# Delta-rule recurrence: the tokens' partition half set by the feature chunk, and state products over four quarters of the array and two PSUM banks

## The reference, cut to what matters

```
sa  = S @ a_t
S   = S * w_t + sa (x) b_t + v_t (x) k_t      # S is 64x64 per head
y_t = S @ r_t
```

## Time and profile before

| what | value |
|---|---|
| median of 3 runs | 1300.0 us (1299.5 to 1301.41) |
| span of the profiled execution | 1299.6 us |
| TensorE busy | 1269.2 us, 98% |
| VectorE busy | 894.2 us, 69% |
| ScalarE busy | 679.4 us, 52% |
| mean granted TensorE clock | 0.995 |
| the stretch of the loop over four chunks | 752.2 to 782.0 us |

### The profile page before, as it was taken

The page is one execution under the profiler, slowest core; times in us unless marked ns, Lnnn a source line. Parts: engine busy times, 40 slices in busy tenths (PEclk is TensorE's granted clock), DMA queues, the critical chain, the costliest instruction groups (busy, mean ns, idle before and its releaser), DMA issues.

```text
span 1299.6 us, 23670 instructions
## 1 busy us (share of the span) xinstructions
PE 1269.2 (98%) x10054; PEld 1098.1 (84%) x10059; DVE 894.2 (69%) x1467; ACT 679.4 (52%) x1228; POOL 83.8 (6%) x103
## 2 busy tenths in 40 slices
PE   9999999999999999999999999999999999999997
PEld 6978888889967888888898997888897987788886
DVE  6886666674685666656898848666668366766666
ACT  6874444463584454544663434444455477445452
POOL 3000500000060000000001600000000000000000
PEclk9999999999999999999999999999999999999999
DMA  9445454544412555553443003654555441455550
GB/s 351 159 184 200 184 190 184 188 188 166 165 62 81 200 195 194 194 195 130 164 161 131 5 36 114 219 193 188 195 194 194 176 161 61 187 194 194 195 194 33
DMA packets 17496, 214.45 MB, mean 165 GB/s; under 512 B 1960, under 2 KB 2128, under 8 KB 4720
## 3 DMA queue, kind: packets, MB, share of 16 engines
q1 hardware_dynamic: 15888, 205.43, 41.9%
q0 software_dynamic: 1504, 7.52, 1.6%
HBM read 211.87 MB, written 1.06 MB: 164 GB/s over the span
## 4 chain that ended last, share of the span: by engine, by line
PE 83%; DVE 9%; ACT 6%; issue 1%; DMA 1%; SPq 0%; DVEq 0%; ACTq 0%
PE psum L696 25%; PE psum L670 14%; PE psum L676 7%; PE psum L486 4%; PE psum L487 4%; PE psum L488 4%; DVE w_low L1996 3%; ACT w_high L1443 2%; PE psum L1054 2%; PE psum L1198 1%; PE psum L585 1%; PE psum L1245 1%; PE psum L1373 1%; PE psum L581 1%; PE psum L577 1%; PE psum L1069 1%
## 5 line engine op out<-in xcount | busy, mean ns | idle before, releaser
L1996 DVE TENSOR_TENSOR w_low<-ring,w_high 128x1024 fp32r<-128x1024 f32 x372 | 443.4, 1227 | 188.5 <-ACT w_high L1443 188.5
L1443 ACT ACTIVATE w_high<-ring 128x1024 fp32r<-128x1024 f32 x372 | 372.7, 1048 | 139.7 <-PE psum L696 105.4
L696 PE MATMUL psum<-w_high,up_split 128*128 128x512 f32 x1024 | 287.6, 391 | 0.8 <-DVE up_split L2151 0.8
L696 PEld LDWEIGHTS psum<-w_high,up_split 128*128 128x128 f32 x1024 | 190.3, 188 | 40.5 <-issue 2.7
L670 PE MATMUL psum<-act_split,w_high 128*128 128x512 f32 x768 | 191.6, 391 | 0.0
L696 PE MATMUL psum<-w_low,up_split 128*128 128x512 f32 x512 | 163.2, 390 | 0.0
L670 PEld LDWEIGHTS psum<-act_split,w_high 128*128 128x128 f32 x768 | 139.6, 189 | 26.0
L1544 ACT ACTIVATE up_split<-work 128x256 fp32r<-128x256 f32 x112 | 46.8, 418 | 159.4 <-DVE work L2144 148.8
L486 PE MATMUL psum<-act_split,w_high 128*128 128x256 f32 x448 | 129.1, 288 | 0.3 <-DVE act_split L2162 0.3
L487 PE MATMUL psum<-act_split,w_high 128*128 128x256 f32 x448 | 126.7, 283 | 0.0
L488 PE MATMUL psum<-act_split,w_low 128*128 128x256 f32 x448 | 126.7, 283 | 0.0
(11 more groups left out here) (360 smaller groups left out, 1873.7 us busy)
## 6 DMA issues: line engine op xcount, KB each, us to landing
ring<-weights SPq DMA_DIRECT2D x95, 2048.0 KB, 7.5
work<-rows POOLq DMA_DIRECT2D x4, 1024.0 KB, 5.1
ring<-weights SPq DMA_DIRECT2D x4, 512.0 KB, 8.4
work<-rows POOLq DMA_DIRECT2D x4, 512.0 KB, 5.4
x<-x_in SPq DMA_DIRECT2D x2, 512.0 KB, 4.7
work<-t_bias POOLq DMA_DIRECT2D x1, 1024.0 KB, 8.4
out<-x SPq DMA_DIRECT2D x4, 256.0 KB, 2.1
con<-consts SPq DMA_DIRECT2D x1, 576.0 KB, 22.0
```

The source lines that it names most:

```text
L696: last = mm(bank(acc[(th, n)]), up_split[:, m, a, P * th:P * th + P], w[:, f], start=start and i == 0, stop=stop and i == len(pairs) - 1, ...
L1443: A(high[:, HIGH_SLOT[name], f], ring[:, n % RING, f], ACT.Copy).then_inc(weights_high, 1)
L1996: V.tensor_tensor(low[:, n % RING, f], ring[:, n % RING, f], high[:, HIGH_SLOT[name], f].bitcast(f32), ALU.subtract).then_inc(weights_spli ...
```

## The change

The partition half of a unit's tokens is now chosen by the feature chunk: `at_half(hf, c)`. In a call that joins features and tokens (g-state, KT, BT, the turn) even chunks use the diagonal quarters and odd chunks the other two, so that one call goes round all four; even chunks write one bank, odd chunks the next (`pair(q)`). Calls whose operands are both on the tokens' side (g-open, u) keep the two diagonal quarters and now alternate over two banks. y keeps one bank: its y-state is split into even chunks, a wait for their completion (`y_even`), and odd chunks, with a further wait (`y_odd`) before y-end. y-open moves behind g-state, y-state moves behind u, and a wait on g-open's own completion (`g_opened`) stands before g-state in chunks 1 to 3 instead of in the odd ones.

`bt` and `kt` are turned by plain 64x64 products, as `vt` was, because pieces beside each other no longer are a pair of neighbouring columns: 64 products a name instead of 31 transposes of 128 columns and two of 64. The Gram matrices are written chunk by chunk; their number, width and alternation of quarters are the same. Readers of a pair of banks use an access pattern of two banks by four pieces of 64.

```diff
-                            if t >= 0:
-                                last = nc.tensor.transpose(got, flat[:, t:t + 2 * CH], cst("diag")[half(hf), :])
...
+                                c, tc = 2 * ((4 * i + j) // NT) + (upper ^ hf), (4 * i + j) % NT
+                                t = (c * NT + tc) * CH
                                 last = mm(psum[half(upper), BANK[q + hf], j * CH:j * CH + CH],
-                                          work[half(hf), src, t:t + CH], cst("center")[half(hf), :], start=True, stop=True)
+                                          work[half(hf), src, t:t + CH], cst(through)[half(hf), :], start=True, stop=True)
...
+                def heads(q, term, first=True, final=True, by_head=False, col=0):
+
                     for c in range(NC):
...
+                        for hf in range(2):
+                            lhsT, rhs = term(half(hf), at_half(hf, c), c)
+                            out, at = at_half(hf, c) if by_head else half(hf), col + c // 2 * CH
+                            last = mm(psum[out, BANK[q] + c % 2, at:at + CH], lhsT, rhs, start=(first and c < 2),
+                                      stop=final, skip_group_check=True)
...
+                def outputs(term, cs=range(NC), first=False, final=False):
+
+                    for c in cs:
+                        for hf in range(2):
+                            lhsT, rhs = term(half(hf), at_half(hf, c), c)
+                            last = mm(psum[half(hf), BANK[y], c * CH:c * CH + CH], lhsT, rhs, start=(first and c == 0),
+                                      stop=final, skip_group_check=True)
...
-                opened = heads(y, [lambda at, hd, c: (rw_gk[at, c, tc, CH:2 * CH], beside(RW_VT, at, hd, c))], True, False)
...
                     pe.wait_ge(sig("state_next"), tc)
...
+                    pe.wait_ge(sig("g_opened"), tc)
+                    heads(q, lambda at, hd, c: (rw_ar[hd, c, tc, 0, :], rw_s[hd, c, :]), False, True)
+                open_bank(y)
+                outputs(lambda at, hd, c: (rw_gk[at, c, tc, CH:2 * CH], beside(RW_VT, at, hd, c)), first=True)
                 read_out(pe, q)
...
+                heads(u, lambda at, hd, c: (rw_y[at, c, tc, :], rw_g[at, c, :]), col=256)
+                if tc:
+                    def from_state(at, hd, c):
+                        return rw_ar[hd, c, tc, 1, :], rw_s[hd, c, :]
+
+                    outputs(from_state, range(0, NC, 2)).then_inc(sig("y_even"), 1)
+                    pe.wait_ge(sig("y_even"), tc)
+                    outputs(from_state, range(1, NC, 2)).then_inc(sig("y_odd"), 1)
...
-                q = TURN[("wkv_g", tc)]
...
-                taken(A(rw_g.rearrange("p c i -> p (c i)"), bank(q), ACT.Copy), q)
+                taken(A(odd_even(rw_g), pair(q), ACT.Copy), q)
```

More of the change, by code:

```diff
@@ L367, in half, with pair, odd_even @@
             return slice(64 * i, 64 * i + 64)
+        def pair(q, at=0):
+            return view(psum[:, BANK[q], at:at + 1], [[512, 2], [CH, NC // 2], [1, CH]])
+        def odd_even(src):
+            return src.rearrange("p (c a) i -> p a c i", a=2)
         def xt(th, n):
@@ L1117, in across, with turned @@
             def across(q, c0, fn, width):
-                n = 1024 // (NT * width)
                 for odd in range(2):
                     open_bank(q + odd)
-                for c in range(n):
-                    for tc in range(NT):
-                        at = (c * 2 + tc // 2) * width
+                for tc in range(NT):
+                    for odd in range(2):
                         for hf in range(2):
-                            lhsT, rhs = fn(half(hf), c0 + c, tc)
-                            last = mm(psum[at_half(hf, tc), BANK[q + tc % 2], at:at + width], lhsT, rhs,
+                            lhsT, rhs = fn(half(hf), c0 + odd, tc)
+                            last = mm(psum[at_half(hf, odd), BANK[q + odd], tc * width:tc * width + width], lhsT, rhs,
                                       start=True, stop=True)
-                        if c == n - 1 and tc >= NT - 2:
+                        if tc == NT - 1:
                             last.then_inc(bank_filled, 1)
[L1132 to L1141, removed]
-                            if t >= 0:
-                                last = nc.tensor.transpose(got, flat[:, t:t + 2 * CH], cst("diag")[half(hf), :])
[L1144 to L1150, removed]
+            def turned(name, src, through="diag"):
                 for i in (0, 2):
@@ L1223, in turn_heads @@
                     for hf in range(2):
-                        last = mm(psum[at_half(hf, tc), BANK[q], c * CH:c * CH + CH], y_norm[half(hf), c, :],
+                        at = c // 2 * CH
+                        last = mm(psum[at_half(hf, c), BANK[q] + c % 2, at:at + CH], y_norm[half(hf), c, :],
                                   cst("diag")[half(hf), :], start=True, stop=True)
@@ L1232, in beside @@
                     hf = hd.start // CH
-                    slot = (c * NT + tc + hf) // 2 % (NC * NT // 2)
+                    slot = c // 2 * NT + tc
                     return work[at, src, (2 * slot + hf) * CH:(2 * slot + hf) * CH + CH]
-                def heads(q, terms, first=True, final=True, by_head=False):
-                    if first:
-                        open_bank(q)
+                def heads(q, term, first=True, final=True, by_head=False, col=0):
                     for c in range(NC):
[L1241 to L1247, removed]
+                        for hf in range(2):
[3 more added lines that the diff above has]
+                                      stop=final, skip_group_check=True)
+                    if final:
+                        last.then_inc(bank_filled, 1)
+                    return last
+                def outputs(term, cs=range(NC), first=False, final=False):
[4 more added lines that the diff above has]
+                                      stop=final, skip_group_check=True)
                     if final:
@@ L1279, in _ @@
                 if tc < NT - 1:
-                    heads(state, [lambda at, hd, c: (beside(RW_BT, at, hd, c), rw_u[at, c, :])], False, True, True)
-                heads(y, [lambda at, hd, c: (rw_gb[at, c, tc, CH:2 * CH], rw_u[at, c, :])], False, True)
+                    heads(state, lambda at, hd, c: (beside(RW_BT, at, hd, c), rw_u[at, c, :]), False, True, True)
+                if tc:
+                    pe.wait_ge(sig("y_odd"), tc)
+                outputs(lambda at, hd, c: (rw_gb[at, c, tc, CH:2 * CH], rw_u[at, c, :]), final=True)
             for n in range(2):
@@ L1846, in _ @@
                 filled(q)
-                taken(A(rw_g.rearrange("p c i -> p (c i)"), bank(q), ACT.Copy), q)
+                taken(A(odd_even(rw_g), pair(q), ACT.Copy), q)
                 q = TURN[("wkv_u", tc)]
                 filled(q)
-                taken(A(rw_u.rearrange("p c i -> p (c i)"), bank(q), ACT.Copy), q)
+                taken(A(odd_even(rw_u), pair(q, 256), ACT.Copy), q)
                 q = TURN[("wkv_y", tc)]
@@ L2594, in heads_out @@
                     filled(q)
-                ins = V.tensor_tensor(raw, bank2(q, NC)[:, c, :], chunks(RW_G)[:, c, t], ALU.mult)
+                ins = V.tensor_tensor(odd_even(raw), pair(q)[:, :, 2 * i:2 * i + 2, :],
+                                      odd_even(chunks(RW_G)[:, c, t]), ALU.mult)
                 if i:
@@ L2613, in _ @@
                     filled(q)
-                    s = rw_s.rearrange("p c i -> p (c i)")
+                    s = odd_even(rw_s)
                     if tc:
-                        taken(V.tensor_tensor(s, s, bank(q), ALU.add), q)
+                        taken(V.tensor_tensor(s, s, pair(q), ALU.add), q)
                     else:
-                        taken(V.tensor_copy(s, bank(q)), q)
+                        taken(V.tensor_copy(s, pair(q)), q)
                     settle()
```

43 lines of the change are left out of this document (18 added, 25 removed).

## The result

The changed kernel takes 1304.98 us (median of 5 runs, 1304.34 to 1306.38), the kernel before 1300.02 on the same chip. The ratio is 1.0036 (95% interval 1.0024 to 1.0049): slower by 5.0 us. The prediction said 1299.7, at most 1301.9, and gave "slower" a chance of 0.08. It was wrong.

What follows compares the result with a forecast made beforehand. The prediction took TensorE's list of work, busy 98% of the span, as the bound. Loop and last turn gain 0.86 us, turning loses 0.51: -0.35 us, so 1299.7 us, with an 8 in 10 range of 1297.4 to 1301.9.

Steps and rivals of the forecast that it cites:

- the turning: Stage of `bt`, `kt`, `vt` before the inverse: `bt` loses 0.37 us, `kt` 0.14, together 0.51 us lost.
- the row behind the price: Profile row of `vt`: first 64 passes release ScalarE after 1.22 us, giving 15.6 ns a pass, 0.50 us a call.
- The Gram matrices: Products behind the turning: same number, width and quarters, so no change in time.
- The loop: The four chunks up to the output projection: ahead by 0.43 us at its end.
- the small steps: Chain from state add to u in chunks 2 and 3, over VectorE and ScalarE: stays at 4.83 and 4.84 us.
- chunk 2, u to state add: In the loop, u and then 3.05 us to the new state: 3.98 us, against 3.65 before.
- Two banks: Rival: two banks are what helps, so g-open and u also run at 0.50 us; 1297.5 us, chance 0.13.
- Dearer waits: Rival: waits on TensorE's own calls cost 0.6 instead of 0.33 us, bank-pair reads take longer; 1301.0 us, chance 0.07.
- The clock: Rival: the granted clock falls in growing gaps between y-open and u in the loop; 1304.9 us, chance 0.02.
- Poorer overlap: Rival: quarters overlap less well in the loop, a call takes 0.80 us; 1304.3 us, chance 0.06.
- the last turn: Turn inside the output projection: takes 0.65 us instead of 1.08, 0.43 less.

Runs made afterwards that it cites:

- m1_pace: A kernel of its own, only stretches of 64x64 float32 products on one, two or four quarters, one or two banks; two quarters took 32.1 to 32.5 us for 1024 passes.
- b_turn_products: The kernel before, with only `bt` and `kt` turned by 64x64 products and its loop untouched: 1305.93 us, ratio 1.0041 to the kernel before.
- a_turn_wide: The changed kernel with `bt` and `kt` turned by 32 transposes of 64x128 again, values not the reference's: 1300.58 us, ratio 1.0003 to the kernel before.
- a_btkt_twice: The changed kernel with each product of `bt` and `kt` done twice into the same place: 1313.97 us, ratio 1.0106 to the kernel before.
- m2_columns: A kernel of its own, stretches of float32 products on four quarters with 64, 16 and 128 moving columns: 27.9, 27.6 and 28.2 us for 1024 passes.
- a_spread: The changed kernel with two bonus head sums between `bt` and `vt` and two between `vt` and `kt`: 1306.97 us, ratio 1.0048 to the kernel before.

## Why the prediction was wrong

**The step that failed** is the turning: "now 128 passes at 15.6 ns and a start, 2.05", and for `kt` "1.00 + 0.28". The first half of that is right: `bt` took 2.12 us. What failed: a pace read from one burst of 64 passes was used for 384 close together, and the sum had no term for the supply of instructions. A packet of instructions lasts 128 passes; the row behind the price is half a packet, and `vt` as a whole one. The sum by its own parts: `bt` +0.45 (forecast +0.37); from `kt`'s start to `vt`'s, 3.86 us against 2.30, +1.56 (forecast +0.14), of which 1.51 is the first gap; `vt` and the Gram matrices, 8.91 us against 6.47, +2.44 (forecast 0), of which 1.22 and 0.84 are the others. "The Gram matrices keep number, width and quarters: nothing" was wrong as well, since a gap left over from the passes ahead fell among them.

**It could have been read.** 188 passes more are 376 instructions, one and a half packets. At 3.46 us for a packet that is 5.1 us of TensorE's time, close to the 4.45 measured. The packets of the kernel before start 3.3 to 4.2 us apart in its loop (754.55, 758.46, 761.79, 765.54), and four small waits of its own, of 0.14 to 0.24 us (before 733.17, 737.29, 745.09 and 764.38), end 1.3 to 1.5 us after one has arrived. The queue was on its page, and was not read:

```profile
q8 instruction: 80, 1.31, 0.4%
```

**The loop.** Calls on four quarters took 0.47 us (forecast 0.50), u and g-open 0.93, the first state copy came 4.54 us after the start (4.48), the state add of chunk 1 after 11.83 (11.98), the small steps 4.83 in chunks 2 and 3 (4.83), chunk 3 from u to the projection 3.77 (3.63). One term was mis-sized: chunk 2, u to state add, 777.80 - 772.79 = 5.01 us where 3.98 was forecast. 0.74 of the 1.03 is the gap just ahead of BT's last passes; y-state and the seams took the rest. The longer gap, 1.18 us in chunk 1, was just covered: y-open runs to 772.95, while ScalarE's copy of g ends at 772.74. That one term turns -0.43 into +0.6.

**The rivals.** Two banks: refuted by m1_pace. Dearer waits: y-state with its wait took 1.22 us in chunk 1 (765.27 to 766.49), forecast 1.27. The clock: 1.00 in both stages. Poorer overlap at 0.80 us a call gave 1304.3, close to the result, and for another reason: no call in the loop cost 0.80. The rule of the Trainium skill that stood beside it (TensorE: Matmul & The Clock Gate, section "Wait — 56ns, not 53.3ns?"), never below about 25 ns from start to start, does not hold here: 128 passes go at 14.7 ns each. Its figure is near what a long stretch shows (27 ns a pass over 1024), but that is the packets' pace and not a pass's. The prediction was right against the rule as worded, and wrong to carry its own row of 64 passes over to hundreds. That 1304.3 came near the result is chance.

What is shown: that the slowdown comes with the passes of `bt` and `kt` (b_turn_products, a_turn_wide), that it scales with their count at the stream's price (a_btkt_twice), and that the waits end when a packet of instructions has come, in the turning, in the loop and in the kernels that do nothing else. What is not shown: what the loop on four quarters would take without these waits; the loop's passes were not varied alone, and no run of that loop is free of them. What sets off a packet, and what passes in the 1.3 us between its arrival and the first matmul, stays open as well.

## What to carry to other kernels

A pace taken from a short burst holds for that burst: before splitting a wide TensorE operation into small ones, multiply out the instructions and set them against what the stream brings (256 in about 3.5 us here), over a stretch of several hundred. Small products on four quarters paid here only where they stood alone, between long matmuls that use few instructions: the last turn did (0.46 us). More instructions in one stage also move the borders of the packets in the stages behind it, as the untouched loop of b_turn_products shows. "issue" idle time that recurs after equal counts, with a packet of the instruction queue that has arrived some 1.3 us before its end, is the mark to look for.

## What the runs showed of the hardware

- TensorE's instructions come in packets of 16 KB, 256 instructions, 128 passes (54 packets for 13824 instructions in m2_columns). With nothing else to wait for, bursts start 3.45 to 4.0 us apart (m1_pace, m2_columns); in no trace here do two packets start less than 3.2 us apart.
- Where TensorE had stood still for over 0.6 us with "issue" in the stages looked at here, it goes on 1.2 to 1.6 us after a packet's arrival (all 41 such waits in nine traces); a packet mostly lasts 0.9 to 1.4 us. Time in which TensorE uses few instructions was not used to fetch ahead (no packet in 6.4 us, a_spread).
- So four quarters give 14.7 ns a pass for 128 passes and 27 ns over 1024, and two quarters 31 ns over 1024: over a long stretch the other two quarters are worth 12%, not half.
- Short matmuls on one pair of quarters gain nothing from alternating two PSUM banks (32.5 us for 1024 in one bank and in two, both at a granted clock of 0.92).
- With 64x128 float32 weights, a plain product costs 56 ns a pass, of which it has two, and a transpose 32 ns, with one pass (m2_columns).
